# The low half of each weight panel written by GpSimd in two instructions of 512 columns instead of one of 1024

## The reference

```python
h = rmsnorm(x, norm_mix);  proj = h @ w_in            # gMLP branch, 8 gated recurrent heads, gates
mix = sigmoid(g_a) * (gmlp @ w_up_a) + sigmoid(g_b) * (hgrn2 @ w_up_b)
x = x + mix @ w_out
x = x + square(relu(rmsnorm(x) @ w_ff1)) @ w_ff2      # 4096 hidden
x = rmsnorm(x, final_norm)
# second block
x = x + short_conv_mixer(rmsnorm(x))                  # 3 x 1024 in, 1024 out
x = x + conv_ffn(rmsnorm(x))                          # 2816 hidden, depthwise convolution, silu gate
x = x + forgetting_attention(...)                     # 16 heads of 64
x = x + conv_ffn(rmsnorm(x))
```

## Time and profile before

| | us |
|---|---|
| median of three runs (2227.18 to 2230.04) | 2229.09 |
| the profiled execution | 2225.64 |
| its span, from the first to the last instruction | 2223.9 |
| TensorE's matmuls busy in it | 2155.3 |
| GpSimd busy in it | 930.7 |
| VectorE busy in it | 990.5 |

### The profile page before, as it was taken

One profiled execution on the slowest core, in us unless ns is written; L12 is line 12 of the kernel. 1 busy time (PEld: TensorE's weight loads), 2 busy tenths in 40 slices (PEclk: granted clock), 3 DMA queues, 4 the chain that ended last, 5 costly groups with the idle time before them and its releaser, 6 DMA issues.

```text
span 2223.9 us, 24400 instructions
## 1 busy us (share of the span) xinstructions
PE 2155.3 (97%) x9662; PEld 1733.4 (78%) x9662; DVE 990.5 (45%) x1588; ACT 797.6 (36%) x1127; POOL 930.7 (42%) x421
## 2 busy tenths in 40 slices
PE   7799999999999999999999999999899999999999
PEld 5677778887888888888888888878666668888887
DVE  4677777633313213535452442421545444514333
ACT  5344445443322223522422222342545444222222
POOL 3544456554444444444444444443211114444444
PEclk9999999999999999999999999999999999999999
DMA  4122121233232322323233232332210102333323
GB/s 168 67 67 67 58 76 57 86 120 118 95 104 95 95 97 94 99 92 103 86 97 103 95 104 87 104 103 77 66 38 30 37 30 94 100 99 95 104 86 114
DMA packets 54977, 194.94 MB, mean 88 GB/s; under 512 B 6096, under 2 KB 6224, under 8 KB 54864
## 3 DMA queue, kind: packets, MB, share of 16 engines
q1 hardware_dynamic: 54864, 193.38, 26.9%
HBM read 191.26 MB, written 2.10 MB: 87 GB/s over the span
## 4 chain that ended last, share of the span: by engine, by line
PE 89%; DVE 8%; ACT 1%; issue 1%; DMA 0%; SPq 0%; POOL 0%; DVEq 0%; POOLq 0%
PE ps L1234 27%; PE ps L1235 26%; PE ps L1236 26%; PE ps L1314 2%; PE ps L1482 2%; DVE arena L853 2%; PE ps L1505 2%; DVE arena L852 1%; PE ps L1242 1%; DVE arena L712 1%; PE ps L1484 0%; PE ps L1513 0%; PE ps L1496 0%; DVE arena L860 0%; DVE x_lo L736 0%
## 5 line engine op out<-in xcount | busy, mean ns | idle before, releaser
L307 POOL TENSOR_TENSOR w_lo<-w_raw,w_hi 128x1024 fp32r<-128x1024 f32 x353 | 852.6, 2419 | 1180.4 <-ACT w_hi L353 1180.3
L1234 PE MATMUL ps<-x_hi,w_hi 128*128 128x512 f32 x1864 | 749.5, 402 | 44.9 <-DVE arena L712 30.0
L1235 PE MATMUL ps<-x_lo,w_hi 128*128 128x512 f32 x1864 | 731.8, 393 | 0.0
L1236 PE MATMUL ps<-x_hi,w_lo 128*128 128x512 f32 x1864 | 731.6, 392 | 0.0
L353 ACT CAST w_hi<-w_raw 128x1024 fp32r<-128x1024 f32 x353 | 366.7, 1041 | 330.4 <-PE ps L1236 323.2
L1234 PEld LDWEIGHTS ps<-x_hi,w_hi 128*128 128x128 f32 x1864 | 354.3, 190 | 131.7 <-issue 49.5
L1235 PEld LDWEIGHTS ps<-x_lo,w_hi 128*128 128x128 f32 x1864 | 354.4, 190 | 76.5 <-issue 5.6
L1236 PEld LDWEIGHTS ps<-x_hi,w_lo 128*128 128x128 f32 x1864 | 353.5, 190 | 75.5
L712 DVE TENSOR_TENSOR arena<-ps,inv_rms 128x512 f32<-128x512 f32 x216 | 149.0, 690 | 487.9 <-PE ps L1236 462.5
L1234 PE MATMUL ps<-hid_hi,w_hi 128*128 128x512 f32 x864 | 337.9, 391 | 5.5 <-DVE hid_lo L741 5.3
L1236 PE MATMUL ps<-hid_hi,w_lo 128*128 128x512 f32 x864 | 337.6, 391 | 0.0
(11 more groups left out here) (163 smaller groups left out, 1599.4 us busy)
## 6 DMA issues: line engine op xcount, KB each, us to landing
w_raw<-in_panels SPq DMA_DIRECT2D x353, 512.0 KB, 3.4
x<-in_xT SPq DMA_DIRECT2D x16, 256.0 KB, 2.7
outT<-x SPq DMA_DIRECT2D x8, 256.0 KB, 2.0
consts<-in_const SPq DMA_DIRECT2D x1, 808.5 KB, 7.7
arena<-in_rows SPq DMA_DIRECT2D x1, 768.0 KB, 9.8
arena<-in_ws SPq DMA_DIRECT2D x1, 256.0 KB, 10.0
params<-in_param SPq DMA_DIRECT2D x1, 112.0 KB, 2.1
```

The lines of the kernel that those rows point to most:

```text
L307: nc.gpsimd.tensor_tensor(w_lo[:, p % RING, :], w_raw[:, p % RING, :], w_hi[:, p % RING, :].bitcast(F), ALU.subtract).then_inc(w_low, 1)
L1234: nc.tensor.matmul(o, wh, hi[:, kt, :], start=(kt == 0), stop=False)
L1235: nc.tensor.matmul(o, wh, lo[:, kt, :], start=False, stop=False)
L1236: ins = nc.tensor.matmul(o, wl, hi[:, kt, :], start=False, stop=(kt == tiles - 1))
```

## The change

`low(p)` writes the panel's low half in two instructions of 512 columns. Both waits stand ahead of the first, and the semaphore is raised by the second alone. Nothing waits between the two.

```diff
@@ -304,8 +304,10 @@
                 pool.wait_ge(w_high, p + 1)
                 if p >= RING:
                     pool.wait_ge(made, p - RING + 1)
-                nc.gpsimd.tensor_tensor(w_lo[:, p % RING, :], w_raw[:, p % RING, :], w_hi[:, p % RING, :].bitcast(F),
-                                        ALU.subtract).then_inc(w_low, 1)
+                for half in (slice(0, D // 2), slice(D // 2, D)):
+                    ins = nc.gpsimd.tensor_tensor(w_lo[:, p % RING, half], w_raw[:, p % RING, half],
+                                                  w_hi[:, p % RING, half].bitcast(F), ALU.subtract)
+                ins.then_inc(w_low, 1)
```

## The result

The kernel with two halves takes 2261.85 us (median of 4 runs, 2258.86 to 2264.96); the one before took 2228.57 beside it (4 runs, 2227.18 to 2230.04). The ratio is 1.0156, 95% interval 1.0141 to 1.0171: slower by 33 us, where 2231.4 was predicted with a range up to 2235.5. The profiled execution took 2260.36 us, its span is 2258.6.

What follows compares the result with a forecast made beforehand. TensorE was taken as the bound (busy 97% of the span, 89% of the chain), with GpSimd mostly having slack. Terms -0.7 + 1.65 + 0.35 + 0.7 + 0.35 = +2.35 us on the 2229.09 median gave about 2231.4, range 2226.0 to 2235.5.

Steps and rivals of the forecast that it cites:

- The turns: Heads: four VectorE spans alternate with 512-column GpSimd instructions, 1.41 us each, 5.64 in place of 5.73; -0.7 us over eight heads.
- The rival that keeps VectorE out for both halves: Heads: both halves act as one longer instruction, stopping VectorE 0.35 us longer each; +5.6 us, 2237.7; chance 7%.
- the one with turns of full length (1.68 us): Heads: the two engines don't overlap at all, four turns take 6.72 us, +1.0 a head; 2240; chance 4%.
- halves are halves: Every panel: the 512-column instruction costs 1.17 us, turns shrink by 0.17 each, late panels cost nothing; about 2226; chance 8%.
- second span between halves: Heads: two VectorE spans slip through between halves, four more hidden per head, -10.9 us; 2220.5; chance 3%.
- The estimate of +0.18: Price of a halved panel, using the Trainium skill's 2048-column figure: 2.1 ns a column, +0.18 us a panel.
- heads 6 to 8, late panel: Two `low` follow the decay work and TensorE waits for the first: +0.55 us each, +1.65 in all.
- end of the heads: The chain goes through one `low` into the first `upa` product: +0.35 us, bounds 0 to 0.44.
- the two convolution gates: Last chunk of each conv_ffn: line 741 lands in the second half, which ends later; +0.35 us twice, +0.7.
- the attention's start, all of it: First query: line 1195 arrives in the second half, +0.35 us, between -1.0 and +0.44; the preceding step was put at 0.
- what the first wins the second loses: Start, layer norm, step ahead of the attention: blocked VectorE instruction followed by another; 0, between -0.3 and +0.3 us each.
- The later end of the second `low` (+0.6): Heads: it falls in GpSimd's 3 us of idle time before its next decay work; no cost was entered.

Runs made afterwards that it cites:

- the kernel with the memsets: The kernel before, whole panels, plus four small GpSimd memsets behind low(p + 5) in each head: 2226.76 us, ratio 1.0002.

## Why the prediction was wrong, step by step

**Right.** The turns: four spans of 1.48 to 1.51 us, one VectorE instruction to one of GpSimd. The rival that keeps VectorE out for both halves and the one with turns of full length (1.68 us) are excluded by them, "halves are halves" (1.17) by a median of 1.29 us, and VectorE gained no second span between halves. None of the four is what happened. GpSimd's busy time, 977 us, lies in the 940 to 1000 that I wrote.

**Right in name, wrong in size.** The instruction has 1.29 us where I took 1.34, but what the sum uses is the difference to a whole panel, and that is half of what I took: 2 x 1.290 less 2.395 is +0.19 us, and over all panels 915.3 less 852.6 us, +0.18 each, where I had +0.35. The estimate of +0.18 that stands beside it in the prediction was the right one. The gain of the turns was put at 0.7 us and came to 0.1: the eviction behind the four spans starts 7.33 us after GpSimd's first work of the head (193.36 less 186.03) where it stood at 7.34 (187.34 before, less 180.00), and TensorE's wait for it fell from 1.24 to 1.22 us a head. The kernel with all but the two middle panels halved measures the other terms:

| place | predicted, us | measured there, us |
|---|---|---|
| heads 6 to 8, late panel | +1.65 | +1.73 |
| end of the heads | +0.35 | +0.74 |
| the two convolution gates | +0.70 | +0.26 |
| the attention's start, all of it | +0.35 | -2.5 |

The first agrees by luck. The panel takes 3.40 us from start to start where it took 2.82, so +0.58 each, but both halves have a VectorE instruction beside them, while without one a panel takes only 0.13 to 0.19 us longer in halves. At the end of the heads the fourth panel's rounding waits for its load until 7.6 us after the first `low` where it was 6.0; I had put the later loads at nothing. At the attention's start I had put the step ahead of it at 0, "what the first wins the second loses". It isn't so: line 1124 of before meets a whole panel and takes 2.73 us, behind a half it takes 1.64, and TensorE's wait for `x_lo` falls by as much, before and then in this kernel:

```profile
PE ps L1234 <- DVE x_lo L736: 5.5, 1, 5.5
```

```profile
PE ps L1240 <- DVE x_lo L742: 4.4, 1, 4.4
```

It is 5.5 us in all eight kernels that have whole panels there and 4.4 in all four with halves. The rest of the 2.5 is 0.6 us of other waits and 0.9 of clock. So outside the heads' decay work the change costs some 2.7 us and gives 2.5 back, and that the total agrees with the kernel before does not make my sum right.

**Wrong.** The step that failed is one clause: "The later end of the second `low` (+0.6) falls in the 3 us before GpSimd's next decay work." It was costed at nothing, by the idle time that it fell in. The duration of that time is right, 2.98 us before and 2.31 after, and the decay work starts no later in the head: 9.44 us after the head's first work in both. But the pause was not only slack: with it shortened, GpSimd's decay gets in at once, VectorE's run is cut into turns, and the head's fourth eviction comes 3.43 us later. I had costed this stretch by one rule, one VectorE instruction per GpSimd instruction, read off, and taken it to hold wherever both are at work. The earlier trace rows said otherwise: of the 56 decays the slowest lasted 2536 ns where the median is 922. An instruction of 256 columns that lasts 2.5 us had waited for something, and the rule of turns had no place for it, since one VectorE instruction of 0.41 us is all that it could wait for. Looking at which of the 56 it was would have shown one in each head, at the start of VectorE's decays, just behind the clause's 3 us.

The prediction named this as what would refute it: a head's length that moves by more than 0.3 us. What I did not have was a rival for it, one in which VectorE's advantage in that stretch is lost. It could have been priced from the rows: in turns the two engines use about 0.9 us per pair (two in 1.80), VectorE alone 0.34, so five instructions that lose their free run cost 5 x 0.56 = 2.8 us a head, on a path where TensorE waits already. Seven or eight heads of that are 20 to 22 us; 24.0 was measured.

**The clock** had no place in my sum either. The stretches at the lower level cost 13.0 us in the profiled execution, half as much again as the waits that they follow. I had priced every wait as if TensorE went on at full rate behind it.

**Who gets in.** A pair of 0.85 and 0.41 us passes in 0.90, so the whole record isn't exclusive, as the prediction said. The Trainium skill ("SBUF — State Buffer", section Who interferes with whom) calls the port pair that the two engines share an exclusive lock; that one holds it for its whole instruction while the other is blocked, it says of VectorE's two-port modes. By the turns the trace agrees, for instructions with two inputs; but if the lock were released after each instruction and went to the engine that waits, GpSimd would have been in after 0.4 us, and in the kernel before it was kept out over five VectorE instructions in every head.

**Open.** What decides whether the waiting GpSimd instruction gets in. Shown: the form of the panel instructions ahead does not; with the last one ending some 0.6 us later it gets in in all eight heads, with 0.3 us later in some of them and not in others. The length of GpSimd's own pause does not either, by the kernel with the memsets, unless the 0.07 us by which the decay work lies otherwise there counts. Not separated: the time since GpSimd's last panel ended, and the place in VectorE's run at which it ended. Neither holds everywhere: the half panel of 7.05 us below was kept out though it started as the half ahead of it ended. The clock is open as well: six of the seven longer waits were followed by the lower level and the seventh, in head 7, was not.

## What to carry to other kernels

Idle time of an engine is slack only as long as the engine it contends with isn't affected by when it ends: shifting GpSimd by 0.6 us, inside its own pause, moved VectorE by 3.4 us and TensorE by as much, and by 5.3 a head with the clock. Read the longest duration of each line beside its median; one that is three times the median is an instruction kept out by another engine, and that engine may have been running free at its expense, an advantage that a small shift can take away. Where the outcome matters, write it into the order by a semaphore instead of leaving it to timing: the wait for the fourth eviction, with the next panel moved ahead of the decays, gave 0.4% on the kernel before and made it indifferent to the change.

## What the runs showed that I had not expected

GpSimd can be kept out for several instructions of VectorE, as long as these follow each other without a gap: 2.53 us in every head before. The longest is in the kernel after, at the start of the attention, a half panel that lasted 7.049 us beside eight VectorE instructions in a row:

```profile
1602.03 10.13 POOL L308 TENSOR_TENSOR w_lo<-w_raw,w_hi 128x512 fp32r<-128x512 f32 x3 [3.37 <-ACT w_hi L355]
...
1603.93 5.37 DVE L738 SCALAR_TENSOR_TENSOR x_lo<-x,params,x_hi 128x512 fp32r<-128x512 f32 x8
```

Three halves took 10.13 us there in place of 3.9, and the other three kernels with halves there have it too (7.03 to 7.04 us). So the same two engines go strictly by turns in one stretch and one keeps the other out in the next. Between the two lies a narrow border: counted from the end of the last panel, GpSimd got in after 2.31 us or less and did not after 2.97 or more, and from 2.644 to 2.650 both occur.

All four pauses of TensorE of 5.7 us (heads 2 to 5 of after) were followed by matmuls at half rate, of the three of 3.45 to 3.47 us (heads 6 to 8) the first and the last, and none of those of 2.3 us before. In these heads the matmuls took 1.4 to 2.8 us longer, which is 2.9 to 5.7 us at half rate.
